# Projections and attention of the last two prompt tiles, moved from the lead-in to run beside the experts of the first two

## What is computed

```python
def block(i):                                   # attention of 128 prompt rows
    w = diff_weights(diff_logits(qb, k5, q_pos, k_pos), lam)   # p[:,0] - lam * p[:,1]
    return jnp.einsum('bhqk,bkhv->bqhv', w, v)
# attn_finish: every head of every row is divided by its root mean square, times subln_g, then @ w_o
# peer_ffn, for each token: 8 heads x 16 experts are chosen out of 16384
    a = jnp.einsum('td,thkd->thk', xt, u_tab[idx])
    hk = g * jax.nn.gelu(a)
    return jnp.einsum('thk,thkd->td', hk, v_tab[idx])
# layer: h = LN(alpha*h + mixer(h)); h = LN(alpha*h + peer(h)); h = h + sigmoid(h Wg) * (p Wp)
```

## Time and profile before

| | us |
|---|---|
| median of 3 runs (3233.61 to 3234.78) | 3233.92 |
| the profiled execution, its own time | 3232.22 |
| its span, from the first to the last instruction | 3230.3 |
| PE / DVE / ACT / POOL busy | 2478.0 / 2258.6 / 2034.9 / 1229.7 |
| mean granted TensorE clock, as a share of full speed | 0.862 |
| window of tile 0, first adds to last | 345.5 to 704.5 |
| window of tile 1 | 704.5 to 1047.0 |

### The profile page before, as it was taken

One profiled execution on the slowest core, in us unless ns is written; L12 is line 12 of the kernel. 1 busy time (PEld: TensorE's weight loads), 2 busy tenths in 40 slices (PEclk: granted clock), 3 DMA queues, 4 the chain that ended last, 5 costly groups with the idle time before them and its releaser, 6 DMA issues.

```text
span 3230.3 us, 42783 instructions
## 1 busy us (share of the span) xinstructions
PE 2478.0 (77%) x13942; PEld 2081.1 (64%) x13942; DVE 2258.6 (70%) x5832; ACT 2034.9 (63%) x3623; POOL 1229.7 (38%) x1100
## 2 busy tenths in 40 slices
PE   9998877767656868887776887888787556586787
PEld 7766676656655667776665866676576545475665
DVE  0663677777688778776767677667667888768755
ACT  0143556676667876566756796556666666667993
POOL 0100344444344444434444434334444444534441
PEclk9997888989877889887898798988798787868999
DMA  5523999999999999999999899999999999999997
GB/s 182 209 105 131 358 405 421 421 406 421 418 421 421 389 420 421 421 418 421 420 419 412 344 421 421 421 421 421 420 419 419 397 400 414 402 378 417 418 421 306
DMA packets 178158, 1237.18 MB, mean 383 GB/s; under 512 B 19918, under 2 KB 23758, under 8 KB 31632
## 3 DMA queue, kind: packets, MB, share of 16 engines
q0 software_dynamic: 156896, 1115.93, 84.0%
q1 hardware_dynamic: 20896, 117.47, 9.1%
q10 hardware_dynamic: 144, 1.05, 0.1%
HBM read 1227.91 MB, written 6.50 MB: 382 GB/s over the span
## 4 chain that ended last, share of the span: by engine, by line
DMA 30%; PE 23%; DVE 21%; ACT 16%; issue 4%; DVEq 3%; ACTq 2%; POOL 1%; SPq 0%
DMA arena<-in_uv,idx 30%; DVE arena L1625 13%; ACT arena L1164 8%; PE acc L1867 6%; PE bank L1668 4%; PE bank L1894 3%; PE bank L1885 2%; ACT L1148 2%; PE bank L1715 2%; PE acc L1864 2%; DVEq L1533 2%; ACT act_w L1157 1%; ACTq L1155 1%; ACT L1154 1%; ACTq L1159 1%
## 5 line engine op out<-in xcount | busy, mean ns | idle before, releaser
L989 POOL DMA_INDIRECT arena<-in_uv,idx x1024 | 1181.4, 1154 | 1641.7 <-PE acc L1867 1411.0
L1867 PE MATMUL acc<-cst,arena 128*128 128x128 f32 x8128 | 1249.1, 316 | 671.5 <-ACT arena L1164 670.8
L1867 PEld LDWEIGHTS acc<-cst,arena 128*128 128x128 f32 x8128 | 1097.0, 164 | 835.5 <-ACT arena L1164 812.6
L1625 DVE CUSTOM_DVE_ANT_0 arena<-arena,h 128x1024 f32<-128x1024 f32 x1024 | 1222.6, 1220 | 353.1 <-DMA arena<-in_uv,idx 348.9
L1164 ACT ACTIVATE arena<-arena,act_w 128x1024 f32<-128x1024 f32 x1032 | 1129.6, 1141 | 37.2 <-issue 2.1
L1154 ACT ACTIVATE act_w<-dots 128x2 f32<-128x2 f32 x520 | 104.8, 201 | 755.5 <-DVE dots L1625 754.9
L1894 PE MATMUL bank<-hT,panel 128*128 128x264 f32 (+2 forms) x1760 | 416.6, 392 | 3.5 <-DMA panel<-in_panels 1.5
L1894 PEld LDWEIGHTS bank<-hT,panel 128*128 128x128 f32 x1760 | 337.1, 200 | 55.6 <-issue 5.0
L1157 ACT ACTIVATE act_w<-act_w 128x1 f32<-128x1 f32 x1040 | 249.9, 287 | 43.4 <-issue 1.1
L1154 ACT ACT_TABLE_LOAD x130 | 166.8, 1283 | 2.0 <-issue 0.2
L1885 PE MATMUL bank<-panel,qT 128*128 128x256 f32 (+1 forms) x640 | 152.9, 394 | 0.0
(11 more groups left out here) (241 smaller groups left out, 2442.9 us busy)
## 6 DMA issues: line engine op xcount, KB each, us to landing
panel<-in_panels SPq DMA_DIRECT2D x94, 1024.0 KB, 9.1
arena<-in_uv,idx POOLq DMA_INDIRECT x1024, 19.9
arena<-in_cache_k POOLq DMA_DIRECT2D x16, 512.0 KB, 5.4
arena<-in_cache_v POOLq DMA_DIRECT2D x16, 512.0 KB, 4.9
arena<-in_panels SPq DMA_DIRECT2D x6, 1024.0 KB, 7.0
arena<-out_y_s POOLq DMA_DIRECT2D x8, 512.0 KB, 6.0
h<-in_h SPq DMA_DIRECT2D x1, 2048.0 KB
out_nv_p<-arena POOLq DMA_DIRECT2D x4, 512.0 KB, 2.9
```

The costliest lines, as they stand in the source:

```text
L989: nc.gpsimd.indirect_dma_start(uv[:, slot_of(e), :], None, uv_dram[layer], bass.IndirectOffsetOnAxis(ids[:, r:r + 1], 0)).then_inc(gathere ...
L1625: V.tensor_tensor_reduce(uv[:, slot_of(e), 0:D], uv[:, slot_of(e), 0:D], x_rows, 1.0, 0.0, ALU.mult, ALU.add, dots[:, G % 2, r:r + 1]).the ...
L1867: m = mm(acc[:, c * P:(c + 1) * P], row, const("ident"), is_transpose=True, start=False, stop=True, skip_group_check=True)
```

## The change

The lead-in does queries, keys, values and attention for tiles 0 and 1 and the samples alone: 16 units of attention in place of 32. The same for tiles 2 and 3 is put into windows 0 and 1 (`others`, and the units placed by the loop over `HEADS`), so the panels of queries, keys and values are loaded twice. Output projection, norm and expert queries of tiles 2, 3 and TB move to window 1. The order of `UNITS` is now tile by tile. The weights that attention makes are no longer normalised: the sum is scaled by ACT, heads are scaled as rows (`o_root`, `o_scale`, `o_back`), and the mean squares come from ACT's sums. The ring has 8 slots for the first 216 gathers. The output projections of tile 0 and tile 1 each load their four panels, and two panels of expert queries are loaded twice.

```diff
-FIRST_RING = 9
-FIRST_GATHERS = 3 * FIRST_RING
+FIRST_RING = 8
+FIRST_GATHERS = 27 * FIRST_RING
-UNITS = [(hd, i) for hd in range(HEADS - 2) for i in range(TB)] \
-    + [(hd, 2 * g + i) for g in range(2) for hd in (HEADS - 2, HEADS - 1) for i in range(2)]
+UNITS = [(hd, i) for i in range(TB) for hd in range(HEADS)]
+LEAD_UNITS = 2 * HEADS
...
+    def queries_and_keys(self, g, p, key):
+        w = self.add_panel("qk", 0, 4 * key + p)
+        made = [self.product(Piece("qk", g=g, f=8 * key + f), w) for f in (2 * p, 2 * p + 1)]
...
+    def lead(self):
...
+        queries = [x for p in range(4) for x in self.queries_and_keys(0, p, 0)]
+        keys = [x for p in range(4) for x in self.queries_and_keys(0, p, 1)]
+        values = [self.values_by(p, (0, 1, TB)) for p in range(4)]
...
+        fill = {0: values[2], 1: values[3], 2: self.rows_of_keys(0), 3: self.rows_of_keys(1),
+                7: self.rows_of_keys(TB) + [Piece("s_new")], 8: folds, 9: [self.product(Piece("s_turn"))],
+                11: [self.o_root[0], self.o_scale[0], Piece("s_probs")], 12: self.o_back[0],
+                13: [self.product(Piece("p_turn"))] + m0[0:2], 14: m0[2:4] + [out[0]],
+                15: a0 + [Piece("ln_acc")], 16: [out[1]] + c0, 17: t0 + [o_turn[0]], 18: q0}
+        lead = queries + self.q_rows + [Piece("lam"), Piece("s_dots")] + keys + values[0] + values[1]
+        for t in range(LEAD_UNITS + 3):
+            lead += (self.score[t] if t < LEAD_UNITS else []) + fill.get(t, [])
+            lead += [self.weigh[t - 1]] * (1 <= t <= LEAD_UNITS) + [self.w_turn[t - 2]] * (2 <= t < LEAD_UNITS + 2)
+            lead += [self.pv[t - 3]] * (t >= 3)
+        lead += [r[0], self.o_root[1], self.o_scale[1], out[2], r[1]] + self.o_back[1] + [r[2], r[3], out[3]] + m1[0:2] \
+            + m1[2:4] + [o_turn[1], Piece("s_sq")] + q1 + [self.s_ms, Piece("s_fix"), r[4], r[5]]
+    def others(self):
+        out = []
+        for p in range(4):
+            out += self.queries_and_keys(1, p, 1) + self.queries_and_keys(1, p, 0) + self.rows_of_last_keys(p)
+            out += self.values_by(p, (2, 3))
+        out += [Piece("v_store", b=b) for b in (2, 3)]
...
+        first_window((0, 1, [r[6]]), (1, 2, [r[7]]), (1, 6, n1 + t1 + q[0:2] + r[8:12]), (6, 14, q[2:] + late), (7, 12, r[12:20]),
+                     (12, 20, r[20:]), (20, 32, r1[:17]), (14, 28, others))
+        bg = self.mix(0, 1)
+        self.at_panel[bg[0].panel] = "rows"
+        bg += self.norm(0, GROUP_TILES[1], False) + self.turn(GROUP_TILES[1], self.ln_of, "norm") + self.features("pq", 0, 1)
+        window(0, 1, (0, 10, r1[17:]), (12.5, 30, bg), (23, 32, r2[:13]))
+        lots = steps[1][3] + steps[2][3]
+        for j in range(HEADS):
+            for b, at in ((2, 34 + 7 * (j // 2) + 3 * (j % 2)), (3, 60 + 2 * j)):
+                u = b * HEADS + j
+                lots[at] += self.score[u]
+                lots[at + 1].append(self.weigh[u])
+                lots[at + 4].append(self.w_turn[u])
+                lots[at + 7].append(self.pv[u])
...
-        window(0, 2, (2, 22, r3), (22, 32, rs[:13]), (0, 32, early))
+        window(0, 2, (0, 12, r2[13:]), (12, 32, r3[:29]), (0, 32, early))
...
+                if plan.at_panel.get(i) == "others":
+                    sp.wait_ge(bank_full, plan.last_first.n + 1)
+                    sp.dma_start(hT[:, :, 0:G_W[0]], h0T[:, :, G_W[0]:SEQ]).then_inc(s_rest, 16)
+                elif plan.at_panel.get(i) == "rows":
+                    sp.wait_ge(a_wT_ps, len(UNITS))
+                    sp.dma_start(h[:, 2:4, :], h0[2 * P:SEQ, :].rearrange("(b p) n -> p b n", p=P)).then_inc(s_h, 16)
```

818 lines of the change are left out of this document (393 added, 425 removed).

## The result

The changed kernel takes 3261.89 us (median of 4 runs, 3255.56 to 3267.08), the kernel before 3234.09 (4 runs). The ratio is 1.0088, 95% interval 1.0076 to 1.0100: slower by 28 us. I had forecast 3222 and given 0.36 to a slower kernel. The profiled execution of the changed kernel has a span of 3258.6 us, 28.3 more than that of before.

What follows compares the result with a forecast made beforehand. The prediction took a lead-in without expert gathers, then DMA moving bytes, as the bounds. Lead-in -84, added bytes +48 and new stalls +27 summed to -9 us, giving 3222 us; the range was 3188 to 3265.

Steps and rivals of the forecast that it cites:

- part 1: Lead-in before the first expert gathers: shorter by 84 us, first adds at about 260 instead of 345.5.
- parts 2 and 3: Behind the lead-in, to the end of tile 1: +48 us for 19.9 MB more bytes, +27 us for new stalls.
- Behind the end of tile 1: Later windows: program nearly unchanged and DMA-bound for 2183 us, the same in both kernels.
- My sign of being wrong: First adds after 285 or before 250, DMA at 420 through experts 112 to 159, or tiles 2 and 3's windows changing over 5 us.
- The clock: Lead-in: PE idles more and runs more of it at the lower clock level, 5 us given back.
- the loop's sum: Attention loop in the lead-in: 16 units and the work filled in between take 94 us, saving 52.
- My bounds: Lead-in: -93 us if values and chain overlap fully, -65 if the tail keeps its length.
- The units' stall: Experts 112 to 159: ACT needs 136 us, DVE 132, DMA 127; 20 us of stall taken.
- Rival A: First 216 gathers: eight slots hold gathers back, 0.3 us each, 3277 us, or 3250 at half price; chance 0.24.
- Rival C: ACT's table loads: a switch costs twice its load, 37 us more, 3259 us; chance 0.05.
- Rival D: Lead-in: tail keeps its 63.5 us and loop waits 12 us longer, -60 us, total 3246; chance 0.05.
- Rivals B and E: Whole kernel: stalls hidden and lead-in at its better bound, 3192 us, chance 0.21; or nothing changes, about 3233, chance 0.10.

Runs made afterwards that it cites:

- e1: Changed kernel with one table entry changed: routing of heads 2 to 7 of layer 1's first tile moved behind the three norms; 3250.28 us, ratio 1.0055.
- e10: As e9, with the lead-in's four products over the cached values standing earlier and further apart; 3219.39 us, ratio 0.9954.
- e9: Changed kernel with e1's edit, tile 1's late routing in lots 16 to 36, tiles 2 and 3's work and output projection four lots later; 3226.95 us, ratio 0.9981.
- e7: Changed kernel with each unit's transposes made five times over in the lead-in, as more work for PE; 3263.17 us, ratio 1.0085.
- e3: Changed kernel with identity in place of the exponentials in units of tiles 2 and 3, so without their table loads; 3258.20 us, ratio 1.0077.
- e5: Changed kernel, tiles 2 and 3: distances' multiple made once per tile, second softmax not subtracted, so less DVE work; 3255.02 us, ratio 1.0067.
- e6: Changed kernel with routing of tile 1's heads 4 to 7 in lots 16 to 48 of window 1, not 0 to 20; 3258.89 us, ratio 1.0078.
- e4: Kernel before with a ring of 8 slots for its first 216 gathers, nothing else changed; 3248.85 us, ratio 1.0052.
- e12: Changed kernel with a ring of 7 slots for the first 217 gathers instead of 8 for 216; 3276.69 us, ratio 1.0135.

## Why the prediction was wrong, step by step

The sum had three terms, and a fourth that I put at nothing. By the profiled executions:

| step | forecast | measured |
|---|---|---|
| part 1, first adds | -84 | -67 (345.5 to 278.4) |
| parts 2 and 3, first adds to gather 256 | +75 | +75 (675.5 to 750.2 us) |
| behind gather 256 | 0 | +21 (span +28.3, gather 256 +7.6) |
| sum | -9 | +28 |

My mark was the last adds of tile 1, not gather 256. They end at 1057.7 (1047.0 before), and what follows takes 2200.9 us where I had said "the same 2183".

**The step that failed most is "Behind the end of tile 1 the program is nearly unchanged ... whatever those windows take, both kernels take".** The change rearranges the routing there as well, in the windows of tiles 2 and 3 and in the next layer. One line of its table moves routing of layer 1's first tile from lots 8 to 26 of its window, with heads 5 to 7 left to do, to lots 0 to 30, with heads 2 to 7. Three norms stand in those first lots. I had read the shift and counted its pieces as equal, without asking what else stood in the same lots. The changed kernel loses 17.5 us there (gathers 520 to 648), and e1 gives 12 of them back with that line alone. Another 6.5 us are lost in the windows of tiles 2 and 3 (gathers 256 to 520, 753.5 us for 747.0), and 3 come back later; no run takes these up. My sign of being wrong named only tiles 2 and 3, where over 5 us were lost indeed, and not the window that cost most.

**Part 1 was mis-sized, -67 for -84.** Its first steps held: queries as rows at 43.6 (forecast 47), last sample score ending at 111.0 (110). The term that was mis-sized is the loop: the units, forecast to take 94 us and end at 205, took 109 and ended at 220 (PE's timeline). The tail then took 58 us, where 52 and the 5 for the clock make 57. In the loop's sum I had no term for the loads of cached values, for which PE never waits from 136 to 345 in the kernel before: a pair of pages is asked for when the product before is done. With 16 units PE waits 5.5 us for them in the loop and 7.5 in the tail, and e10, which removes these waits, brings the adds forward by 7.5 us against e9. The clock, for which I gave back 5 us, fell to 0.71; e7 shows that PE's idle time is behind it and that a mean of 0.81 makes the other matmuls 9.3 us shorter, but not how much of that lies on the path. Some 9 us of the 17 stay open, with the clock as the first candidate. My bounds, too, did not follow from their terms: values and chain fully overlapped, 12 + 8 us, would make -104 and not -93, and a tail at its full length, 12 us, makes -72 and not -65.

**Parts 2 and 3 were right in their sum by luck: two errors cancel.** Bytes cost 29 us, not 48. I counted the added panels and stores nearly right (13 panels more, not 14), but not that the first eight gathers, issued by 265 at the latest, would be mostly in before the stretch begins: its gathers brought 253.3 MB, where they had brought 258.9. Idle time cost 44 us, not 27. The stall before tiles 2 and 3 was 19.6 us of PE and, by bytes, 12 us of DMA from 439 to 508, where I had 7 for it: the second load of the tokens, in packets of 1 KB between those of the gathers, took 25.9 us, not a panel's 9.5, and the panel stood behind it. The units' stall is about the size that I said (gathers 112 to 160 take 152.7 us where my 127 and 20 make 147), but for another reason: I had put it down to ACT. e3 takes 15 us from ACT and gains no gather; e5 and e6 take work from DVE and gain 6 and 11 us. Neither sum was short: from 614 to 767, which is these gathers, ACT was busy 129 us (I had 136) and DVE 122 (132), and the stretch took 153. What failed is the step from the larger sum to the time. DVE and ACT feed each other, and their waits add to the busy time: DVE waits 13 us for the routing's exponential and only 3 for gathers, ACT waits 11 us for dots and 5.5 for logits.

**Rival A, the ring,** has a true part: e4 prices eight slots at 17 us in the kernel before, e12 the step to seven at 15 more. I had put this term at nothing beside the 27. Its mechanism is not a steady price: the eight slots are enough in plain lots (421 GB/s from 813 to 918) and cannot bridge a dense one. The sign that I had named for it, POOL waiting for a slot with DMA idle, is there: 28.1 us of POOL's wait ahead of 469.7, with DMA at 0.09 from 459 on. Of 44 us more idle time the late load and the dense units hold most. How much would be left with eleven slots was not tried, since the three others hold data of tiles 2 and 3, so the shares of the ring and of the dense lots in these 44 us are not told apart.

**Rival C** did not come about: ACT does not stand still ahead of a load. This group of the changed kernel's page has 142 loads with 2.0 us of idle time ahead of them in all:

```profile
L1154 ACT ACT_TABLE_LOAD x142 | 182.2, 1283 | 2.0
```

The Trainium skill, "ScalarE: Activation LUTs", section "What ACT_TABLE_LOAD costs", adds some 1380 ns of drain to each load. These rows do not bear it out, and e3, without the units' loads, gained no gather.

**Rival D's** number for part 1 (-60) was nearer than mine, and its reason half right: the loop took 15 us longer than said, the tail 1. **Rivals B and E** did not come about.

## What to carry to other kernels

When a planner's table is edited, compare lot by lot what each engine gets, also in parts that the change "only" renumbers: changes to five lines of the table were worth 35 us here (e9), and with the lead-in's order a change that lost 28 us became one that wins 13, with the same work. An engine whose busy share is 80% can still hold the others back: look whether it ever waits for the resource that is taken for the bound (dots that wait for gathers), since where that wait is gone, something else is on the path. And when two engines feed each other, do not take the larger of their busy sums for the time. A gain at one place holds only if the next dense place can take it, so shifts are to be tried together as well as alone. Count issues against the same ring, or a shorter ring looks like lost time.
